# Two layers of a diffusion backbone with a mixture of experts on one core: the last modulation chunks moved behind the first expert pass, and the joins around it reordered

## The reference, cut to what matters

```python
for l in range(2):                       # layer 0: attention, layer 1: pooling mixer
    sh1, sc1, g1, sh2, sc2, g2 = silu(cond) @ ada_w[l] + ada_b[l]   # 6 vectors of 1024, per condition
    h = rms_norm(x, norm_mix_g[l]) * (1 + sc1) + sh1
    x = x + g1 * mixer(h)
    h = rms_norm(x, norm_ffn_g[l]) * (1 + sc2) + sh2
    x = x + g2 * moe(h)                  # top 1 of 4 groups, then top 2 of its 8 experts
# moe: sum over the 2 chosen experts e of  weight * (silu(h @ gate_e) * (h @ up_e)) @ down_e
# mixer of layer 1: per group of 256 columns, (mean over a centred window - h) @ w_pool, * pool_scale
```

## Time and profile before

| | us |
|---|---|
| median of 3 runs | 871.26 (866.87 to 872.73) |
| the profiled execution | 872.78 |
| its span, first to last instruction | 870.70 |
| PE busy in it | 731.4 (84%) |
| DVE busy in it | 352.0 (40%) |
| DMA moved in it | 294.42 MB, mean 338 GB/s |

### The profile page before, as it was taken

One profiled execution on the slowest core, in us unless ns is written; L12 is line 12 of the kernel. 1 busy time (PEld: TensorE's weight loads), 2 busy tenths in 40 slices (PEclk: granted clock), 3 DMA queues, 4 the chain that ended last, 5 costly groups with the idle time before them and its releaser, 6 DMA issues.

```text
span 870.7 us, 12882 instructions
## 1 busy us (share of the span) xinstructions
PE 731.4 (84%) x4560; PEld 405.2 (47%) x4560; DVE 352.0 (40%) x830; ACT 141.3 (16%) x342; POOL 175.7 (20%) x275
## 2 busy tenths in 40 slices
PE   4899989999976999999889763877899999797760
PEld 3333433467834655555445431735555545344430
DVE  2222548642245244444333332556244444333233
ACT  3111154531352000000000001544000000000000
POOL 0000400000002143333323120001133343332220
PEclk9999999999986899999999996787799999999995
DMA  9999849841864899999999953976699999999935
GB/s 345 428 435 422 234 151 415 315 194 47 362 269 164 323 418 419 419 416 420 417 418 422 420 238 130 419 325 205 214 421 416 421 415 423 419 422 419 414 131 217
DMA packets 41979, 294.42 MB, mean 338 GB/s; under 512 B 10872, under 2 KB 12336, under 8 KB 22864
## 3 DMA queue, kind: packets, MB, share of 16 engines
q1 hardware_dynamic: 29248, 275.51, 77.7%
q0 software_dynamic: 10880, 13.26, 5.0%
q10 hardware_dynamic: 1808, 5.06, 1.4%
HBM read 293.24 MB, written 22.02 MB: 362 GB/s over the span
## 4 chain that ended last, share of the span: by engine, by line
PE 64%; DMA 19%; SPq 6%; DVE 5%; issue 3%; ACT 1%; POOL 0%; POOLq 0%; DVEq 0%
PE bank L1578 21%; PE bank L1602 9%; DMA ring<-in_moe_w_in 8%; PE bank L1326 7%; PE bank L1251 4%; DMA ring<-in_moe_w_out 4%; PE bank L1425 3%; DMA ring<-in_ada_w 3%; PE bank L1556 3%; SPq L392 2%; DMA adaw<-results 2%; PE bank L1433 2%; PE bank L1468 2%; PE bank L1385 2%; DMA adaw<-in_ada_w 1%
## 5 line engine op out<-in xcount | busy, mean ns | idle before, releaser
L1578 PE MATMUL bank<-ring,qkv 128*64 128x256 f32 x1440 | 175.2, 397 | 23.2 <-issue 11.6
L1578 PEld LDWEIGHTS bank<-ring,qkv 128*64 128x64 f32 x1440 | 110.2, 143 | 74.5 <-issue 22.4
L547 POOL DMA_INDIRECT results<-adaw,scur x65 | 67.8, 1043 | 286.4 <-DVE adaw L1124 253.2
L1101 DVE COPY qkv<-bank 128x512 f32<-128x512 f32 x64 | 44.3, 692 | 194.5 <-PE bank L1556 174.3
L805 ACT ACTIVATE qkv<-bank 128x128 f32<-128x128 f32 x64 | 17.8, 278 | 445.7 <-PE bank L1578 411.1
L1602 PE MATMUL bank<-ring,qkv 128*64 128x512 f32 x360 | 87.1, 604 | 1.2 <-DVE qkv L1113 0.8
L537 POOL DMA_INDIRECT adaw<-rows,gcur x57 | 59.2, 1039 | 44.3 <-issue 28.0
L1326 PE MATMUL bank<-ring,hT 128*128 128x512 f32 x144 | 63.5, 596 | 1.3 <-DVE hT L879 1.3
L1113 DVE COPY qkv<-bank 128x128 f32<-128x128 f32 x64 | 18.7, 292 | 75.7 <-PE bank L1587 74.5
L1122 DVE SCALAR_TENSOR_TENSOR adaw<-qkv,wcur 128x512 f32<-128x512 f32 x64 | 48.1, 752 | 2.3
L1124 DVE SCALAR_TENSOR_TENSOR adaw<-bank,wcur,adaw 128x512 f32<-128x512 f32 x64 | 48.1, 751 | 2.3
(11 more groups left out here) (236 smaller groups left out, 839.7 us busy)
## 6 DMA issues: line engine op xcount, KB each, us to landing
ring<-in_moe_w_in SPq DMA_DIRECT2D x44, 2048.0 KB, 25.2
ring<-in_moe_w_out SPq DMA_DIRECT2D x45, 1024.0 KB, 33.3
adaw<-in_ada_w SPq DMA_DIRECT2D x16, 2048.0 KB, 11.2
adaw<-in_moe_w_in SPq DMA_DIRECT2D x10, 2048.0 KB
ring<-in_ada_w SPq DMA_DIRECT2D x8, 2048.0 KB, 12.1
xT<-in_moe_w_in SPq DMA_DIRECT2D x10, 1536.0 KB
hT<-in_moe_w_out SPq DMA_DIRECT2D x10, 1024.0 KB
ring<-in_attn_w_qkv SPq DMA_DIRECT2D x3, 2048.0 KB, 36.1
```

Source lines behind the costliest of these rows:

```text
L547: pool.indirect_dma_start(res, bass.IndirectOffsetOnAxis(ap=scur[:, p, :], axis=0), yout[:, p], None, bounds_check=res_limit, oob_is_err=F ...
L1101: V.tensor_copy(xgT[:, p], bank[2][:, :]).then_inc(xgT_ready, 1)
L1578: last = T.matmul(bank[p][64 * a:64 * a + 64, 0:2 * P], xk[:, k % 4, k // 4], w[k // IN_X if b > RING else 0][:, k % IN_X if b > RING else ...
```

## The change

- Chunks 21, 22 and 23 are no longer loaded in attention and in the router of layer 0. SP issues them at the end of layer 0's pass, behind the extra tile's weights, once the gate and up products of tiles 27, 30 and 31 are done, into ring slots 3, 0 and 1. PE multiplies them behind the extra tiles, and `set_copy(3)`, `vectors(3)` and the last part of the bias addition follow there. DVE's additions of set 2 (layer 0's gate 2 and the first part of layer 1's vectors) move ahead of the router.
- Expert 4's gate and up weights are issued in attention, behind expert 3's.
- POOL clears its buffer after chunk 20 and not after chunk 23.
- In both layers PE makes the offsets (`over_mm`) ahead of `rows_by_token(4)` and `(5)`.
- `result` and `extra` do the copy and the gates' share before they wait for the down products.
- `total` becomes two parts with a semaphore per half: x += half 0, then x += half 1. In layer 0 bands are scaled between these parts.
- PE turns x (`raw`) ahead of the window products of the same tile, once x is summed, and ACT copies the first tile's turned x ahead of the second tile's square.

```diff
+        TAIL, LEFT, RIGHT, HIGH0, HIGH1, RING3, RING0, RING1 = range(8)
+        ada_place += [ring[:, b, 0:KD * ACH] for b in (3, 0, 1)]
+        ADA_AT = [TAIL, LEFT, RIGHT, HIGH0, HIGH1] + [(i + 2) % 3 for i in range(5, 2 * NCH - 3)] + [RING3, RING0, RING1]
...
-            for i in range(8, 2 * NCH - 1):
+            for i in range(8, 2 * NCH - 3):
                 load_ada(i)
...
                 if l == 0:
+                    sp.wait_ge(ada_mm, 20)
                     load_out(l, 3, 3, s_wout[3])
...
+                    load_in(l, RING, RING, s_win[RING])
                     sp.wait_ge(pv_mm, NU // 4)
...
                     sp.wait_ge(ada_vec, 2)
-                    sp.wait_ge(ada_mm, 22)
...
-                if l == 0:
-                    load_ada(2 * NCH - 1)
...
+                if l == 0:
+                    for i, s in ((21, NE - 5), (22, NE - 2), (23, NE - 1)):
+                        sp.wait_ge(gu_mm, s + 1)
+                        load_ada(i)
...
-                    pool.wait_ge(ada_mm, 24)
+                    pool.wait_ge(ada_mm, 21)
...
                     square(0)
-                    square(1)
                     raw(0)
                     raw(1)
+                    square(1)
...
-                    dve.wait_ge(down_mm, l * NE + s + 1)
...
                     V.scalar_tensor_tensor(yout[:, p], gdiff, wcur[:, p, 1:2], glat, ALU.mult, ALU.add).then_inc(y_order, 1)
                     dve.wait_ge(y_order, s * 2 + (l * NE * 2 + 2))
+                    dve.wait_ge(down_mm, l * NE + s + 1)
...
+            def first_part(l, t):
                 dve.wait_ge(x1_copied, l * 6 + 6)
-                order(V.tensor_tensor(parts[t][:, 0], parts[t][:, 0], parts[t][:, 1], ALU.add))
-                V.tensor_tensor(xtok[:, t, :], xtok[:, t, :], parts[t][:, 0], ALU.add).then_inc(x_sum, 1)
+                dve.wait_ge(s_xin[t][0], l * 16 + 16)
+                order(V.tensor_tensor(xtok[:, t, :], xtok[:, t, :], parts[t][:, 0], ALU.add))
+
+            def second_part(l, t):
+                dve.wait_ge(s_xin[t][1], l * 16 + 16)
+                V.tensor_tensor(xtok[:, t, :], xtok[:, t, :], parts[t][:, 1], ALU.add).then_inc(x_sum, 1)
...
             scales(1, 1, 8)
+            dve.wait_ge(ada_vec, 4)
+            vectors_of(3, 1, 4 * KD + KD // 2, 6 * KD)
...
-                rows_by_token(4)
-                rows_by_token(5)
-                if l == 0:
-                    ada(23)
...
                 last.then_inc(over_mm, 1)
+                rows_by_token(4)
+                rows_by_token(5)
...
+                    for i in range(SETS[3], 2 * NCH):
+                        ada(i)
```

More of the change, by code:

```diff
@@ L238, in build @@
         SETS = (0, 4, 10, 21, 2 * NCH)
-        SET_BANK, VECTOR_BANK = (0, 1, 2, 0), (2, 0, 1, 1)
+        SET_BANK, VECTOR_BANK = (0, 1, 2, 0), (2, 0, 2, 2)
         def set_of(i):
@@ L328, in build @@
             "xg_mm", "xgT_ready", "gu_mm", "silu_ready", "hid_ready", "hid_mm", "hidT_ready", "down_mm", "y_ready"))
-        s_xin = [sem(f"s_xin{t}") for t in range(TT)]
+        s_xin = [[sem(f"s_xin{t}{k}") for k in range(2)] for t in range(TT)]
         std_t = sem("std_t")
@@ L446, in _ @@
                     sp.dma_start(bands, bands_in).then_inc(s_bands, 16)
-                    sp.wait_ge(ada_vec, 4)
+                    sp.wait_ge(ada_vec, 3)
                 sp.wait_ge(x1_mm, l * 6 + 6)
@@ L590, in extra @@
                         gather(j + NE, 0, x_idx[l], j * 2, xs_g[l])
-                    scatter(j + NE, 0, x_idx[l], j * 2 + 1, x_y[l], j + 1, xs_y[l])
+                    scatter(j + NE, 0, x_idx[l], j * 2 + 1, x_moved[l], j * 6 + 6, xs_y[l])
                     pool.wait_ge(xs_y[l], j * 16 + 16)
@@ L821, in _ @@
                 extra_tiles(act, n_extra, extra)
+                if l == 0:
+                    set_copy(3)
             for t in range(TT):
@@ L859, in modulation, with vectors_of @@
             def modulation(n, l, a, b):
-                cols = bank[VECTOR_BANK[n]][:, l * 2 * NMOD + 2 * a * KD:l * 2 * NMOD + 2 * b * KD]
-                m = mods[:, l, a * KD:b * KD, :]
+                vectors_of(n, l, a * KD, b * KD)
+            def vectors_of(n, l, a, b):
+                cols = bank[VECTOR_BANK[n]][:, l * 2 * NMOD + 2 * a:l * 2 * NMOD + 2 * b]
+                m = mods[:, l, a:b, :]
                 order(V.tensor_tensor(m, cols.rearrange("p (m c) -> p m c", c=2),
-                                      bias[:, l, a * KD:b * KD].unsqueeze(2).to_broadcast([P, (b - a) * KD, 2]), ALU.add))
+                                      bias[:, l, a:b].unsqueeze(2).to_broadcast([P, b - a, 2]), ALU.add))
             def scales(l, i, first):
@@ L1175, in extra @@
                     V.tensor_copy(wcur[:, 0, :], wm[:, bass.ds(j + NE, 1), :].rearrange("p a c -> p (a c)"))\
-                        .then_inc(x_order[l], 1)
-                    dve.wait_ge(x_order[l], j * 2 + 1)
+                        .then_inc(x_moved[l], 1)
+                    dve.wait_ge(x_moved[l], j * 6 + 4)
                     V.scalar_tensor_tensor(yout[:, 0], gdiff, wcur[:, 0, 1:2], glat, ALU.mult, ALU.add)\
-                        .then_inc(x_order[l], 1)
-                    dve.wait_ge(x_order[l], j * 2 + 2)
+                        .then_inc(x_moved[l], 1)
+                    dve.wait_ge(x_moved[l], j * 6 + 5)
+                    dve.wait_ge(x_down[l], j + 2)
                     V.scalar_tensor_tensor(yout[:, 0], bank[4][:, :], wcur[:, 0, 0:1], yout[:, 0], ALU.mult, ALU.mult)\
-                        .then_inc(x_y[l], 1)
+                        .then_inc(x_moved[l], 1)
                 extra_tiles(dve, n_extra, extra)
             norm_dve(0, 0, 4, 3, lambda k: hT[:, k, 0:CTX])
+            dve.wait_ge(ada_vec, 3)
+            modulation(2, 0, 5, 6)
+            vectors_of(2, 1, 0, 4 * KD + KD // 2)
+            V.memset(ss[:, 17:18], 0.0).then_inc(mods_ready, 1)
             router(0)
@@ L1210, in _ @@
             V.memset(ss[:, 18:19], 0.0).then_inc(mods_ready, 1)
-            total(0, TILES_BACK[0])
-            total(0, TILES_BACK[1])
+            first_part(0, TILES_BACK[0])
+            second_part(0, TILES_BACK[0])
+            first_part(0, TILES_BACK[1])
             scale_tile(0)
-            total(0, TILES_BACK[2])
+            second_part(0, TILES_BACK[1])
+            first_part(0, TILES_BACK[2])
             scale_tile(1)
+            second_part(0, TILES_BACK[2])
             scale_tile(2)
@@ L1229, in _ @@
             for t in range(TT):
-                total(1, t)
+                first_part(1, t)
+                second_part(1, t)
         @block.tensor
@@ L1613, in step @@
                     hidden_T(s, q % 2)
+                pe.wait_ge(mods_ready, 3 + l)
                 rows_T(0, 0, old=False)
@@ L1672, in _ @@
                     for n in range(TT):
+                        if n < 2:
+                            pe.wait_ge(x_sum, n + 1)
+                            raw(2 * n)
+                            raw(2 * n + 1)
                         pe.wait_ge(band_ready, n + 1)
```

43 lines of the change are left out of this document (12 added, 31 removed).

## The result

The changed kernel takes 866.57 us in the median of 18 runs (861.47 to 869.66), the kernel before 870.62 on the same chips (18 runs, 866.87 to 875.37): a ratio of 0.9939, interval 0.9921 to 0.9958. It gains 4 us where 13 were forecast. Two later groups of runs gave 864.42 against 870.20 (0.9929, 0.9904 to 0.9954) and 865.33 against 870.95 (0.9943, 0.9917 to 0.9969). The profiled execution took 861.67 us with a span of 859.7, at the low end of its runs, so the two traces show 11.1 us of difference, which is more than the medians bear out.

The account below looks back on a forecast made before the run. Each expert pass was taken to last as long as its bytes take, so gains lie around the passes; terms -10.8 + 0.5 + 1.1 + 0.6 + 0 - 0.95 - 2.2 - 1.2 = -12.95 gave 859.5 us, range 853 to 866.

Parts of the forecast that it names:

- Router of layer 0, -10.8: Turned logits to first gather in layer 0: chunk stall and slow DVE scaling go; -10.8 us, between -9.0 and -11.5.
- Everything is as in layer 1 then: Layer 0's router, stall and slow scaling gone, should match layer 1's 21.35 us from turned logits to first gather.
- rival A: First expert pass bound by something whose start doesn't move, so the head start is lost; about 870 us, chance 0.04.
- Offsets ahead of the last rows, +0.5 and +1.1: Both routers: PE's wait for DVE is exposed, +0.5 us in layer 0; later `keep` copies, +1.1 in layer 1.
- Chunks in the tail, +0.6 and 0: End of layer 0's pass: chunks slow the last weights by 0.6 us; scatter and read-back sharing engines taken as 0.
- So the chunks just fit: End of layer 0's pass: with chunk 23, DVE may add to x from 540.5 us, against 540.57 before.
- Share -0.95: Extra tile of layer 0: copy and gates' share move into DVE's wait, bringing the scatter 0.95 us earlier.
- halves, windows and turning -2.2: Behind layer 0's pass, first addition to third scaling gets shorter; -2.2 us, between 0 and -3.5.
- End of layer 1, -1.2: Last tile of layer 1: first addition goes ahead of the second half's landing; -1.2 us (0 to -1.3).
- Clearing at its new place, 0: POOL's clearing, now in attention near 178 us, costs between nothing and 0.9 us; taken as nothing.
- C: Rival: edits between and behind passes do nothing or harm, only layer 0's router gains; -7.1, so 865.7 us, chance 0.16.
- B: Rival: tail of layer 0's pass, chunk 23 lands 15 us later; 874.8 us, chance 0.04, plus 0.04 for middle near 865.

Follow-up runs that it names:

- chunks_only: Changed kernel with offsets, gates' share, halves and turning of x back in their old places, leaving only the chunk move; 865.64 us (0.9924).
- hold_expert5: Changed kernel with expert 5's gate and up load in layer 0 held until the fourth gather has landed; 862.96 us (0.9896 of before).
- after_again: Changed kernel unchanged, one further execution for a second trace; 862.08 us.
- joins_only: Changed kernel with chunks, set 3, expert 4's load and the clearing as before, all other edits kept; 863.48 us (0.9903).
- joins_layer1_old: joins_only with the offsets behind the last turned rows again in layer 1, new order in layer 0 only; 861.88 us (0.9884).
- halves_only: Kernel before with only gates' share, halves and turning; offsets and chunks as before; 868.47 us (0.9969).
- held versions: Versions of the changed kernel with expert 5's load in layer 0 held until the gathers have landed; 856.96 to 862.96 us.
- offsets_late: Changed kernel with the offsets behind the last turned rows again in both layers; 864.10 us (0.9923).
- offsets_only: Kernel before with one edit, offsets ahead of the last turned rows in both layers; 863.12 us (0.992).
- hold_rows_first: Changed kernel with the edits of hold_expert5 and offsets_late together; 858.59 us (0.9865), and 859.69 us (0.987) when run again.
- before_again: Kernel before unchanged, one further execution for a second trace; 871.21 us.
- after_timed_2: Changed kernel unchanged, timed again for a fourth trace as partner of a version without the chunk loads; 865.33 us (0.9943).
- the pairs' partners: The same kernels with the chunk transfers kept, beside versions without them; 864.42, 859.69 and 865.33 us.

## Why the prediction was wrong, and where it was right

The kernel got faster, as forecast, and the stall went; but the gain was a third to a half of what was forecast: 859.5 us and at most 866, against 866.57. By the stretches, term by term:

- **Router of layer 0, -10.8: right as far as it went.** With the old order of the offsets, the gather starts 21.4 us behind the logits (chunks_only; 32.2 before): -10.8. The stall and the slow scaling went as said. The term ended at the start of the gather, and what ends the stretch is its landing.
- **The step that failed: "Everything is as in layer 1 then", with layer 1 measured only as far as the start of the gather.** The sum took every us by which the gather starts earlier as a us for the rows. I had named expert 5's load only in rival A, as one that "might now load in vain", and not as one that meets the gather. It now goes out 0.12 us behind the gather's start, and the rows are turned 7.5 us behind that start, 5.0 before: +2.5. The 5.0 was PE's own work, 1.7 us of it set 3's columns (282.46 to 284.17), which are gone; with the load held the rows take 3.3 (hold_expert5). So the load costs 4.2 us of what was there to gain. The kernel before showed a sign of it in layer 1, where the load is out ahead of the gather and PE waited 2.11 us for the rows.
- **Offsets ahead of the last rows, +0.5 and +1.1: the ordering costs as said, and the clock comes on top.** In layer 0 the gather starts 1.7 us later than with the old order (23.1 in three traces of four against 21.4; 22.0 in the first). Of this, DVE's start is +0.4 (12.49 us behind the logits in after_again, 12.07 in chunks_only, the counts taking 2.77 us in both), as forecast. The other 1.26 is the first table at the lower clock, 2.79 us and not 1.53. The forecast had that as "about 1.3 us more" on the low side of its first term and gave it nothing. `keep`, ahead of the table, wasn't what the table waited for in layer 0. In layer 1 it is: there the table starts 7.0 to 7.1 us behind DVE's start, not 6.1, and the router costs 1.9 us more (joins_only against joins_layer1_old). The first trace is faster in layer 0 because its counts took 1.69 us and not 2.77.
- **Chunks in the tail, +0.6 and 0: too low.** Chunk 23 landed at 525.67, 5.4 us behind the down products of the extra tile, against the 4.7 of the forecast (535 less 530.3). The error lies elsewhere, in "So the chunks just fit". I had measured that against the first addition of before (540.57), and in the same sum let the share bring the read-back forward by 0.95. Once that was counted, no slack was left. On top of it the scatter landed 1.5 to 1.8 us later beside the chunks, and in the first trace chunk 23's products ran at a granted clock of 0.53 (3.61 us, not 1.92). Together 2.2 us by the tail's stretch: 68.7 in the mean of the four traces, 66.5 in the mean of the five with the same joins and neither a chunk there nor the hold. Single pairs say 0.7 to 2.8, and the medians nothing or 2.7.
- **Share -0.95, halves, windows and turning -2.2: right.** Without chunks the read-back is issued 1.0 us sooner, at 4.4 and not 5.4; first addition to third scaling takes 11.6 us, where 11.75 was worked out. halves_only gives 3.6 for the two.
- **End of layer 1, -1.2:** measured -0.9.
- **Clearing at its new place, 0: right.** It runs at 176.43 for 1.80 us, and DVE's instructions beside it last as long as their like in the kernel before (0.69, 0.42, 0.16 and 0.48 us).

The sum: -10.8 + 2.5 + 1.7 + 1.9 + 2.2 - 3.6 - 0.9 = -7.0, and -7.5 by the stretches. The medians say -4 to -6. What remains, 1 to 3 us, stays open: the traced executions of the kernel after lay low among their runs, and the others left no trace.

Of the signs that the prediction named, the extra tile's weights (9.67 us earlier), the third scaling (11.6 us) and the one addition at the end came. The first gather was to come 21 to 22.5 us behind the logits; it did so at 22.0 in the first trace and not at 23.1 in the other three. Two slips stand in the working: the bounds of its terms add to -17.25 and -2.95, not -18 and -4, and PE's free time in the earlier trace rows is a sixth and not a fifth.

Of the rivals, C had the nearest time, 865.7, though the edits between the passes did gain. A fell, since the pass moved with its start (pass 0 is 229.7 to 231.1 us in all but the held versions). B fell, since chunk 23 landed 0.7 us later than forecast and not 15, counted from the extra tile's down products.

The larger lesson was in no rival: moving the chunks and moving the offsets are two remedies for one stall. Beside the chunk move, the new order has nothing left to hide: it costs in both routers by the traces, in the medians only once the load is held (858.59 against 862.96), since offsets_late gave no gain. Beside the new order, the chunk move gains nothing in the router (30.6 us in joins_only, 30.4 after) and costs in the tail. offsets_only at 863.12 us and the whole change at 864.42, not told apart, say it in one comparison. The fastest version with all its transfers was hold_rows_first, at 858.59 and 859.69 us (0.9865 and 0.987), better than both kernels: chunk move, old order, and the load held.

## What to carry to other kernels

When a wait goes, list every instruction behind it in its queue, loads above all: they start earlier too, and may meet the one transfer that now decides. Where two edits cure the same stall, price each with the other already made. A transfer put into the gap ahead of an event must be measured against that event's new time, after all other terms of the sum.

## What the runs showed of the hardware

- A small gather is slowed by a large load begun beside it, to more than twice its time. Start of the gather to rows turned: 3.3 us with the load held (hold_expert5, no wait for the rows), 7.5 with 2 MB issued 0.12 us behind it (PE waits 4.1), 8.64 with them issued 0.17 us ahead of it (offsets_late). With the load 3.49 us ahead, in layer 1 of the kernel before, it was 4.88 with a wait of 2.11. The 5.0 of its layer 0 is PE's own work and no time of a gather. By the Trainium skill, *DMA: Bandwidth & Descriptors*, section "Queues, rings and completion order", the engines alternate between the rows that have work, packet by packet. No run here tells alternation from standing in line: the scatter of the extra tile was seen to land 0.7 us behind chunk 23 in two traces (525.7 and 526.4, 528.7 and 529.4), which fits both. If they alternate, it isn't free: 1.74 or 1.75 us of waiting without chunks in the three traces that leave them out, 3.29 to 3.54 with them in the kernel after, 2.90 and 4.48 in the two held versions.
- The same matmuls of the first table in the router of layer 0 took 1.53 us at a granted clock of 0.99 (chunks_only) and 2.79 at 0.50 (after). Reordering eight matmuls ahead of it decided which, in twelve traces of twelve; no run shows by what rule.
- PE's clock in the first stage differs between executions of the same code. The two rows below are of before and of before_again (start to end, time, busy time and instructions of PE, PEld, DVE, ACT and POOL, granted clock, DMA share, GB/s):

```profile
36.00:56.00 20.00, 19.58 (x57) 8.23 (x58) 4.69 (x17) 2.17 (x4) 0.00 (x0) 1.00 1.01 430
```

```profile
36.00:56.00 20.00, 18.68 (x53) 7.86 (x52) 5.36 (x21) 2.17 (x4) 0.00 (x0) 0.84 1.00 428
```

  The same 32 matmuls took 13.97 us in the one and 16.17 in the other. It isn't all that spreads the first stretch (244.1 to 251.5 us): hold_rows_first and after_timed_2 both had a clock of 1.00 up to 140 us but for one dip to 0.96, and reached the logits at 244.1 and 246.8. Single traces must be compared by stretch.
- Without the chunks' transfers pass 1 was 231.7 to 232.9 us in three traces, against 230.2 to 231.7 in the pairs' partners. No run here explains it.
